# A fifth probability tile, and turns, lower parts and value products one score slot further behind their scores

## The reference

```python
# native sparse attention: 16 heads of 64, two streams of keys (selected, window), and a compressed one
s = jnp.einsum('bqghd,bgqnld->bghqnl', qc, kg) * scale
p = masked_softmax(s, mask)                 # causal
o = g[:, :, 0] * o_cmp + g[:, :, 1] * o_slc + g[:, :, 2] * o_win
# forgetting attention: 16 heads, a bias F_q - F_k
s = jnp.einsum('bqhd,bkhd->bhqk', qc, k) * scale
s = s + Fq[..., None] - F[:, :, None, :]
p = masked_softmax(s, mask)                 # causal
```

## Time and profile before

| | us |
|---|---|
| median of 3 runs | 1458.62 (1458.53 to 1458.86) |
| the profiled execution, its own time | 1458.66 |
| its span in the trace | 1456.9 |
| PE busy | 1441.6 (99%) |
| DVE busy | 1030.2 (71%) |
| ACT busy | 906.7 (62%) |
| POOL busy | 491.4 (34%) |
| mean granted clock of TensorE | 0.999 |

### The profile page before, as it was taken

One profiled execution on the slowest core, in us unless ns is written; L12 is line 12 of the kernel. 1 busy time (PEld: TensorE's weight loads), 2 busy tenths in 40 slices (PEclk: granted clock), 3 DMA queues, 4 the chain that ended last, 5 costly groups with the idle time before them and its releaser, 6 DMA issues.

```text
span 1456.9 us, 22913 instructions
## 1 busy us (share of the span) xinstructions
PE 1441.6 (99%) x7490; PEld 1223.3 (84%) x7490; DVE 1030.2 (71%) x2431; ACT 906.7 (62%) x1912; POOL 491.4 (34%) x578
## 2 busy tenths in 40 slices
PE   9999999999999999999999999999999999999998
PEld 7888888888888888888888888888888888888887
DVE  6837888888888874444576488888888887643444
ACT  6636888778878752223364487788788887522234
POOL 2403664555556420000022155554565555000000
PEclk9999999999999999999999999999999999999999
DMA  9232212212122143333453321212122121433332
GB/s 284 75 101 59 58 47 57 59 45 59 45 59 53 51 130 92 96 101 90 111 184 89 101 53 51 59 44 59 47 57 58 45 58 46 144 92 104 92 101 91
DMA packets 201627, 118.29 MB, mean 81 GB/s; under 512 B 9305, under 2 KB 195889, under 8 KB 201009
## 3 DMA queue, kind: packets, MB, share of 16 engines
q1 hardware_dynamic: 199120, 107.49, 27.1%
q0 software_dynamic: 1728, 8.66, 1.6%
q10 hardware_dynamic: 672, 0.83, 0.2%
HBM read 110.54 MB, written 6.42 MB: 80 GB/s over the span
## 4 chain that ended last, share of the span: by engine, by line
PE 84%; ACT 6%; DVE 4%; issue 4%; POOL 1%; DVEq 0%; POOLq 0%; ACTq 0%
PE acc L1888 54%; PE turned L1962 6%; PE o_pair L1987 6%; PE scores L1945 3%; PE scores L1947 3%; PE turned L2214 2%; ACT q_fox L891 2%; PE scores L2214 1%; ACT prob L963 1%; ACT w_hi L842 1%; PE turned L2138 1%; DVE prob L1447 1%; PE misc L2007 1%; DVE q_fox L1359 1%; PE scores L1888 1%
## 5 line engine op out<-in xcount | busy, mean ns | idle before, releaser
L1888 PE MATMUL acc<-u_lo,w_hi 128*128 128x512 f32 x968 | 380.1, 393 | 0.0
L1888 PE MATMUL acc<-u_hi,w_hi 128*128 128x512 f32 x968 | 379.4, 392 | 0.0
L1888 PE MATMUL acc<-u_hi,w_lo 128*128 128x512 f32 x968 | 378.8, 394 | 0.0
L1272 DVE TENSOR_TENSOR w_lo<-w_raw,w_hi 128x1024 fp32r<-128x1024 f32 x184 | 231.1, 1256 | 126.8 <-ACT w_hi L842 125.8
L963 ACT ACTIVATE prob<-prob,row_max 128x384 f32<-128x384 f32 (+3 forms) x384 | 215.3, 561 | 119.7 <-DVE row_max L1447 113.8
L842 ACT ACTIVATE w_hi<-w_raw 128x1024 fp32r<-128x1024 f32 x184 | 193.4, 1052 | 151.4 <-PE acc L1888 95.3
L765 POOL TENSOR_SCALAR prob<-prob,row_inv,gates 128x256 f32<-128x256 f32 (+3 forms) x256 | 184.0, 720 | 215.1 <-DVE row_inv L1454 214.4
L1888 PEld LDWEIGHTS acc<-u_hi,w_lo 128*128 128x128 f32 x968 | 182.0, 188 | 34.0
L1888 PEld LDWEIGHTS acc<-u_hi,w_hi 128*128 128x128 f32 x968 | 181.8, 188 | 33.5 <-issue 0.2
L1888 PEld LDWEIGHTS acc<-u_lo,w_hi 128*128 128x128 f32 x968 | 181.9, 188 | 32.1 <-issue 0.2
L1447 DVE CUSTOM_DVE_ANT_0 prob<-scores,causal 128x384 f32<-128x384 f32 (+3 forms) x384 | 184.4, 480 | 19.2 <-PE scores L1947 18.2
(11 more groups left out here) (330 smaller groups left out, 2562.9 us busy)
## 6 DMA issues: line engine op xcount, KB each, us to landing
w_raw<-in_w_in_dram SPq DMA_DIRECT2D x140, 512.0 KB, 3.7
w_raw<-in_w_proj_nsa_dram SPq DMA_DIRECT2D x16, 512.0 KB, 3.8
w_raw<-in_w_proj_fox_dram SPq DMA_DIRECT2D x16, 512.0 KB, 3.8
w_raw<-in_w_out_dram SPq DMA_DIRECT2D x16, 512.0 KB, 3.8
x_scratch<-xT POOLq DMA_DIRECT2D x2, 2048.0 KB, 8.7
xT<-x_scratch POOLq DMA_DIRECT2D x2, 2048.0 KB, 8.8
x_nat<-in_x_dram SPq DMA_DIRECT2D x4, 512.0 KB, 6.5
c_w<-in_cmp_w_k_dram SPq DMA_DIRECT2D x4, 512.0 KB, 5.5
```

The lines of the kernel that those rows point to most:

```text
L1272: dve.tensor_tensor(w_lo[:, par, :, 0:width], w_raw[:, par, :, 0:width], w_hi[:, par, :, 0:width], ALU.subtract).then_inc(w_lo_done, 1)
L1888: ins = pe.matmul((bank or acc[par])[0:width, :], own_w, rhs, start=(n == 0), stop=(n == 23))
```

## The change

The ring of probability tiles gets a fifth member: `v_raw`, a tile of the same size that lies idle during the cycles. Since 24 is no multiple of 5, the ring now goes by the absolute number of the step. The pairs of turns are formed the other way round: in an odd slot s the steps s - 4 and s - 3 are turned (an odd step first), in an even one the lower parts of s - 5 and s - 4 are made, and every value product stands five slots behind the last step of its attention. The narrow products stay in their slots, and so does work with a slot of its own. `Plan` is told of the new places and so spreads the projection matmuls anew. The signal `kf_first` comes after the second copy of the keys rather than the first.

```diff
-SM_RING = 4
+SM_RING = 5
-LAG_SCALE, LAG_TURN, LAG_PT, LAG_PV = 1, 2, 3, 4
-LAG_NARROW = LAG_PV + 2
+LAG_SCALE, LAG_PV = 1, 5
-def both(s, lag):
-
-    return (lag + 1, lag) if (s - lag) % 2 else ()
+def turn_lags(s):
+
+    return (4, 3) if s % 2 else ()
+
+
+def low_lags(s):
+
+    return () if s % 2 else (5, 4)
+
+
+def narrow_lags(s):
+
+    return (7, 6) if s % 2 else ()
...
-            for lags, cost in (((-1,), self.score_cost), (both(s, LAG_TURN), self.turn_cost),
-                               (both(s, LAG_PV), self.value_cost)):
+            for lags, cost in (((-1,), self.score_cost), (turn_lags(s), self.turn_cost),
+                               ((LAG_PV,), self.value_cost)):
...
-            prob = sb("prob", [P, SM_RING, T])
+            prob = sb("prob", [P, SM_RING - 1, T])
...
+        def prob_of(ring):
+
+            return v_raw if ring == SM_RING - 1 else prob[:, ring, :]
...
-                    t, qt, ring = pair.s0 + s, pair.at(s)[1], s % SM_RING
+                    t, qt, ring = pair.s0 + s, pair.at(s)[1], (pair.s0 + s) % SM_RING
...
-                        if h == 0 and rows == own(0):
+                        if h == 0 and rows == other(0):
                             ins.then_inc(kf_first, 1)
...
-                    for lag in both(s, LAG_TURN):
+                    for lag in turn_lags(s):
...
-                    for lag in both(s, LAG_PT):
+                    for lag in low_lags(s):
...
-                    if ending(s, LAG_PV):
-                        extra.setdefault(s, []).append(lambda now=ending(s, LAG_PV): value_step(*now))
+                    if ending(s, (LAG_PV,)):
+                        extra.setdefault(s, []).append(lambda now=ending(s, (LAG_PV,)): value_step(*now))
```

More of the change, by code:

```diff
@@ L227, in bass_trunk @@
         row_inv = sb("row_inv", [P, SM_RING])
-        sb("up_to_2_kb", [P, 32])
+        sb("up_to_2_kb", [P, 29])
         u_hi = sb("u_hi", [P, KT, T], F32R)
@@ L754, in scale_step @@
             def scale_step(pair, s):
-                (a, qt), ring = pair.at(s), s % SM_RING
+                (a, qt), ring = pair.at(s), (pair.s0 + s) % SM_RING
                 h, _, branch = pair.atts()[a]
-                p = prob[:, ring, 0:P * (qt + 1)]
+                p = prob_of(ring)[:, 0:P * (qt + 1)]
                 pool.wait_ge(s_inv, pair.s0 + s + 1)
@@ L779, in body @@
                     at(10, lambda: gate_output(Pair(False, l, i - 1, cycle.g)))
-                at(CYCLE_STEPS + 1 if cycle.last else 16 + LAG_PV + 3, lambda: gate_output(cycle.nsa))
+                at(CYCLE_STEPS + 1 if cycle.last else 23, lambda: gate_output(cycle.nsa))
                 if cycle.last:
@@ L960, in exp_step @@
                     t = pair.s0 + s
-                    ring, width = s % SM_RING, P * (pair.at(s)[1] + 1)
+                    ring, width = t % SM_RING, P * (pair.at(s)[1] + 1)
                     act.wait_ge(s_max, t + 1)
-                    act.activation(prob[:, ring, 0:width], prob[:, ring, 0:width], ACT.Exp,
+                    act.activation(prob_of(ring)[:, 0:width], prob_of(ring)[:, 0:width], ACT.Exp,
                                    bias=row_max[:, ring:ring + 1], scale=-1.0,
@@ L981, in body @@
                     at(1, lambda: lower_half(before, 0))
-                    at(LAG_PV + 1, lambda: lower_half(before, 1))
-                at(8 + LAG_PV + 1, lambda: lower_half(nsa, 0))
-                at(16 + LAG_PV + 1, lambda: lower_half(nsa, 1))
+                    at(5, lambda: lower_half(before, 1))
+                at(13, lambda: lower_half(nsa, 0))
+                at(21, lambda: lower_half(nsa, 1))
                 if cycle.last:
@@ L1446, in max_step @@
                     apart(dve)
-                    dve.tensor_tensor_reduce(prob[:, ring, 0:width], scores[bank][:, first:first + width],
+                    dve.tensor_tensor_reduce(prob_of(ring)[:, 0:width], scores[bank][:, first:first + width],
                                              causal[:, T - width:T], -SCALE, BIG, ALU.add, ALU.min,
@@ L1452, in invert_step @@
                     dve.wait_ge(s_exp, pair.s0 + s + 1)
-                    ring = s % SM_RING
+                    ring = (pair.s0 + s) % SM_RING
                     dve.reciprocal(row_inv[:, ring:ring + 1], row_sum[:, ring:ring + 1]).then_inc(s_inv, 1)
@@ L1471, in body @@
                     at(2, lambda: head_output(before, 0))
-                    at(LAG_PV + 2, lambda: head_output(before, 1))
-                at(8 + LAG_PV + 4, lambda: head_output(nsa, 0))
-                at(16 + LAG_PV + 2, lambda: head_output(nsa, 1))
+                    at(6, lambda: head_output(before, 1))
+                at(16, lambda: head_output(nsa, 0))
+                at(22, lambda: head_output(nsa, 1))
                 if cycle.last:
@@ L2026, in body, with ending @@
                     extra.setdefault(slot, []).insert(0, what)
-                def ending(s, lag):
-                    for n in (s - each for each in both(s, lag)):
-                        now = cycle.step(n) if n < CYCLE_STEPS else None
+                def ending(s, lags):
+                    for lag in lags:
+                        now = cycle.step(s - lag) if s - lag < CYCLE_STEPS else None
                         if now and now[0].ends(now[1]):
@@ L2050, in body @@
                     narrow = scored and not scored[0].nsa and scored[0].starts(scored[1])
-                    turns = [cycle.step(s - lag) for lag in both(s, LAG_TURN) if s < plan.slots and s - lag < CYCLE_STEPS]
+                    turns = [cycle.step(s - lag) for lag in turn_lags(s) if s < plan.slots and s - lag < CYCLE_STEPS]
                     turns = [step for step in turns if step]
```

4 lines of the change are left out of this document (2 added, 2 removed).

## The result

The changed kernel took 1578.31 us (median of 6 runs, 1575.81 to 1584.24), the kernel before 1458.55 in the same job (6 runs, 1458.38 to 1458.86): a ratio of 1.0828, 95% interval 1.0808 to 1.0848, 119.8 us slower. The forecast was 1528, with a range to 1550: the direction and the place were right, the size was not. The profiled execution took 1575.81 us, with a span of 1574.1 and a mean granted clock of 0.983; the span before was 1456.9, so the trace has 117.2 us to explain.

The account below looks back on a forecast made before the run. PE is the bound, limited by how early DVE and ACT come through their in-order queues. 1458.66 + 40.6 (boundary) + 42 (slots 11 and 12) - 12.9 (old waits) = 1528.4 us; range 1478 to 1550, the forecast case's own 1505 to 1545.

Parts of the forecast that it names:

- three places: New PE waits per cycle: 2.9 us at slot 0 (cycle boundary), 1.7 at slot 11, 1.3 at slot 12.
- rival (b): Clock also falls to 1.2 GHz after the boundary's 2.9 us wait, 14 times, 20 us more: 1548 us; chance 0.11.
- The boundary: Slot 0's value product waits 2.9 us for a late lower part, 14 times: 40.6 us.
- Slots 11 and 12: PE waits 1.7 us at slot 11's turn and 1.3 at slot 12's value product, 14 cycles: 42 us.
- Old waits that go: PE's present waits vanish: 0.74 us in 12 middle cycles, about 2 in each first cycle; 12.9 us off.
- my list of unit ends that move: Ends of projection units 0, 1, 3 go from slots 4, 8, 18 to 5, 10, 19, moving work hung on them.
- The layers' ends: Tail after a layer's last cycle has one slot more but no more matmuls: costs nothing.
- Rival (a): Only one of the waiting places decides; with the boundary alone 1486 us; chance 0.17.
- Rival (c): DVE's idle time absorbs the moved work and old waits go, 8.9 to 23.7 us, say 17: 1442 us; chance 0.07.

Follow-up runs that it names:

- e2: Changed kernel with z_tanh and z_silu one slot earlier, ahead of the cycle boundary; 1531.85 us, ratio 1.0500.
- e11: e2 with the projection matmuls of slots 4 to 13 dealt as in e7; 1470.48 us, ratio 1.0079.
- e4: Changed kernel with the forgetting queries' round one slot later (slot 8) and its subtraction two later (slot 10); 1592.41 us, ratio 1.0911.
- e7: Changed kernel at its new lags, but the planner counts turns and values at the old lags, so projection matmuls keep their old slots; 1461.29 us, ratio 1.0016.
- e5: Changed kernel with ten unread matmuls in slot 0 ahead of the waiting value product, in every cycle but each layer's first; 1554.29 us, ratio 1.0654.
- e10: e7 with the last cycle's hung work put in exactly the slots of the kernel before; 1453.09 us, ratio 0.9962.

## Why the prediction was wrong

The places and their order were right. Two steps of the sum failed, by about 20 us each in the profiled run: it counted PE's waits beyond three places at nothing, and it left the clock out as rival (b). The account of the profiled run's 117.2 us, by the starts of the compressed scores that open each cycle:

- *The boundary, forecast 40.6:* 2.97 us between starts in 12 crossings and 3.20 in the two into a last cycle, 42.1. The term holds, and so does the mechanism (e2).
- *Slots 11 and 12, forecast 3.0 x 14 = 42:* in 12 cycles 1.6 to 1.8 and 1.0 to 1.4 us between starts, in each layer's first cycle only 1.2 and 0.6; 38.7 in all. Holds in the middle cycles (e11, and e4 by where its waits went).
- *Old waits that go, forecast 12.9:* e7, where they go and nothing new comes, has cycles that are 9.8 us shorter in these 14, 0.7 in each middle one and 0.65 in each first. The forecast had 0.74 and 2. Its 2 came from the 17.0 of the earlier trace rows, read as PE's loss, though 14.6 of it is idle time of the weight loads; PE's own is 2.4.
- *Missing from the sum, the first failed step:* with the clock kept (e5), the 14 cycles take 91.3 us more than before; the terms above give 42.1 + 38.7 - 9.8 = 71.0. The other 20.3 are slot 17 (0.7 in 12 cycles, 8.3), a wait of 0.6 in each first cycle, and small losses elsewhere. I looked at two deadlines beside the boundary and counted the rest at nothing, and my list of unit ends that move (0, 1 and 3) left out unit 2, which goes from slot 13 to 14. So slot 15 of DVE, where a split, kf and q_raw came together, was not costed.
- *The clock, rival (b), chance 0.11, the second failed step:* the falls came at 11 of 14 crossings, 20.7 us in this run (its cycles less those of e5) and 24.0 between the medians. I had the wait and the row that says what such a wait does, and priced it as another case in place of a term. A fall of 3.4 us cost 1.4 to 1.8 us, one of 6.8 us 2.3 to 2.5, near the 1.45 forecast or above it; the 20 of rival (b) was a fair price.
- *The layers' ends, counted at nothing:* 2.4 us between the landmarks and 3.6 behind the second layer's last cycle opens, less 0.9 by which the first cycle opens earlier: 5.1.

42.1 + 38.7 - 9.8 + 20.3 + 20.7 + 5.1 makes 117.1. Neither failed step alone explains the miss: e5, without falls, still takes 1554.29, 26 us above the forecast, and the forecast with the clock added was 1548. Rival (a) fell: the waits added up. When e2 shortened the boundary's, those of slots 11 and 12 stayed (1.44 and 1.06 us of idle time, against 1.4 to 1.6 and 0.9 to 1.3), and when e11 took these away, the total fell by as much. Rival (c) was half right: the longer lag does take the old 0.7 away, but only where the helpers' work stays in its slots (e7, e10), for 5.7 us, not 17. With the idle time filled (e5) the clock is 1.000; that agrees with the Trainium skill, "TensorE: Matmul & The Clock Gate", section on what is actually happening, by which the lower level comes after idleness. The Trainium skill, "Perfetto Trace Analysis", section Optimization Strategy, says that a repeated gap can mean too few buffers. A fifth `prob` tile alone (e1) left the gap as it was, with cycles of 50.88 us; but the gap waits for one of the two `turned` banks, and a third of those was not tried.

What stays open: some 11 us of small losses (0.8 us per cycle) were not tested one by one, nor which part of e11's edit cleared which of slots 11, 12 and 17. The longer lag and the new pairing of turns were only ever run together.

## What to carry to other kernels

When a pipeline's lag is changed, its planner may move everything that hangs on it: change the lag and the placement apart, since here the lag with its new pairs was worth 0.7 us per cycle and the placement cost 8% of the whole. Before hanging a helper's job on an in-order engine, list what stands behind it there up to the next deadline of the bounding engine, and check all deadlines of the cycle, not the first two found. If a wait as long as those after which the clock fell cannot be removed, put the bounding engine's own work in it.

## What was not expected of the hardware

Waits of the same length had different outcomes. Idle for 2.81 us from the matmul at 282.4 on, PE kept its clock at 1.00; idle for 2.80 us from that at 339.9 on, it lost it at about 342.3, some 2.3 us after its last start. Over the 11 falls this distance goes from 2.3 to 4.2 us, and in five the clock fell when PE had been at work again for 0.2 to 1.0 us; at the end of the span before it held for 2.9 us after PE's last matmul. In e4 a wait of 1.90 us, with one of 0.66 three us ahead of it, brought falls too, while the waits of 1.4 to 1.6 us at slot 11 of the changed kernel brought none. So the fall is not told by one wait's length alone, and runs of the same kernel scatter by 8 us (1575.81 to 1584.24, clocks 0.983 to 0.976, the slower the lower) where those with a steady clock scatter by under 1 (e2, e5). Once fallen at 342.3, the clock stayed at 1.2 GHz for 6.8 us though PE worked again after 0.9 of them (343.14). And work that has no use made the kernel 24 us faster (e5).
